# Second block's attention as six two-head jobs between weight units, bias as tiles from DRAM

## The chip, the cores and the metric

One of the cores of a Trainium2 chip runs the kernel. The metric is the device time of one execution in microseconds; less is better.

## What is computed

Two different transformer blocks of two layers each run on 256 rows of 1024 numbers, all in fp32. The first has four kinds of attention and an MLP. The second, in which the change lies, projects x by `w_in_2` (11,648 columns) and has two mixers side by side. One is attention in three groups of six heads of 64 (windows 128, 512, 2048, dilations 1, 4, 16) with a T5 bias by distance:

```
s = einsum(q, k) * 64 ** -0.5 + bias[bucket(distance)]; masked outside window and dilation
o = softmax(s) v per group; y_a = sum over groups of softmax(lse over groups) * o
```

Since the groups are merged by their log denominators, the three groups of a head are one softmax over 3 x 256 keys. The other mixer is retention in four heads (query and key 256, value 512), whose queries and keys are rotated by position. Both mixers are projected and gated, then come `w_out_2`, LayerNorm, a SwiGLU and another LayerNorm.

## The kernel before

**Weights in three products.** TensorE works in fp32r. A weight unit is 512 rows by 512 columns (1 MB). SP loads it into one of four buffers `raw`, ScalarE copies it to `whi` (helper `hi`, line 1007), VectorE subtracts to `wlo` (`lo`, line 1386), and TensorE multiplies for four blocks of k and two row tiles: x high and x low by `whi` (lines 573, 574), x high by `wlo` (line 579), 24 matmuls of 512 columns. A chunk of w_in is two units into a pair of PSUM banks; VectorE adds the input bias and stores it (`project`, line 1744). `whi` and `wlo` have two buffers each, so hi of a unit waits for the unit two before it.

**Order.** Each engine has its program written out by hand, with counting semaphores (`Tally`). In a layer of the second block TensorE turns x (`first_chunk`), makes chunks 0 to 5 of w_in (queries, keys, part of the values), turns queries and keys (line 598, 36 transposes), makes chunk 6, and then runs attention alone: `run_jobs` with `JOBS2`, 12 jobs, one for each head and row tile m. Job step q has `logits2` of job q, `job_turn` of job q - 1 and `job_outputs` of job q - 2. Then YA, the attention's output, is turned, and the ten units of chunks 7 to 11 follow (7 to 10 are the queries and keys of retention). Then retention's blocks are turned (`T2_RET`).

**A job.** For each of three groups TensorE multiplies a 64 row block of queries with (m + 1) x 128 keys (line 720), and adds the bias by two matmuls against a reversed identity, `flip` (line 723). Its operands, the high and low part of a skewed read of the bias rows in DRAM, are loaded by SP for each job into `YH` and `YL`, behind a wait for the logits two jobs before. VectorE takes the row maximum (line 1425) and negates it (line 1427), ScalarE does the exponential from PSUM (line 1007), TensorE turns the probabilities into PSUM tile `T` (two banks, line 598), VectorE copies them (line 1448), TensorE multiplies with the values into `A` (line 641), and VectorE divides by the sum (lines 1455, 1457).

**Retention's rotation** is `rotate` on VectorE (lines 1773 to 1780), after each of chunks 7 to 10, with its scratch `RTR` in the arena.

**Setup.** One matmul (line 662) and some VectorE operations make the 18 bias rows from `rel_bias_2`; ScalarE writes them to DRAM early. GpSimd loads constants, `decay` among them, and rotates some heads of the first block. In the first block the logits (line 691) of a job come from four heads, with neighbours in different row halves, the transposes have line 598 and the value matmuls line 646.

## Time and profile before

| | |
|---|---|
| Runs, median of 3 | 2182.11 us (2181.06 to 2182.19) |
| The profiled execution, its own time | 2180.04 us |
| Its span | 2178.2 us |
| Mean granted TensorE clock | 0.922 |
| Busy, share of the span: TensorE, VectorE, ScalarE, GpSimd | 94%, 55%, 40%, 3% |
| DMA, mean over the span | 158 GB/s |

Engines are PE (TensorE, with PEld for its weight loads), DVE (VectorE), ACT (ScalarE), POOL (GpSimd) and SP. The granted clock is a share of full speed. Busy TensorE is not TensorE at its best: its matmuls take longer at a lower clock. An fp32 matmul is two records in the trace, an fp32r matmul one; in the first block's groups "x8" are four fp32 matmuls. Numbers behind the bar of a group are idle time before it and what ended it.

### The profile page before, as it was taken

To read this page: it belongs to the slowest core of one execution; us is meant where nothing else is said; L and a number is where in the kernel's file an instruction comes from. 1 tells how busy PE (TensorE), PEld (TensorE's weight loads), DVE (VectorE), ACT (ScalarE), POOL (GpSimd) and SP (SyncE) were. 2 spreads that over 40 slices of the span, in tenths; PEclk is the share of its full clock that TensorE was granted. 3 is DMA by queue.
4 is the path that set the end of the run, shared out by engine and by line. 5 is a ranking of instruction groups with operands and counts; after the bars stand their busy time and mean duration, and the time that the engine had idled before them with its cause. 6 is when DMAs were issued, how large, how long until landed. Compare 5 with 4: busy or idle time off the path is not lost.

```text
span 2178.2 us, 26315 instructions
## 1 busy us (share of the span) xinstructions
PE 2043.5 (94%) x9270; PEld 1672.1 (77%) x9270; DVE 1193.5 (55%) x1360; ACT 873.9 (40%) x997; POOL 62.1 (3%) x88
## 2 busy tenths in 40 slices
PE   4998999899899998999999989997999999998997
PEld 3886888687778877877877778886877887787885
DVE  3675555557555555433766564445532757555455
ACT  3544444456253444311345434443321335443442
POOL 2210000022000000000000000000000000000000
PEclk9987999999799999956999999998965999999998
DMA  5413555452245544643655645554644555654553
GB/s 192 148 52 121 177 189 173 156 168 90 77 155 180 192 150 157 207 87 108 209 177 174 208 145 169 179 183 165 205 113 126 173 175 174 193 187 132 177 180 115
DMA packets 214819, 345.17 MB, mean 158 GB/s; under 512 B 13355, under 2 KB 82219, under 8 KB 214721
## 3 DMA queue, kind: packets, MB, share of 16 engines
q1 hardware_dynamic: 213440, 342.10, 49.4%
q8 instruction: 58, 0.95, 0.2%
q0 software_dynamic: 384, 1.31, 0.2%
q10 hardware_dynamic: 897, 0.49, 0.1%
q14 instruction: 40, 0.33, 0.1%
HBM read 342.74 MB, written 1.12 MB: 158 GB/s over the span
## 4 chain that ended last, share of the span: by engine, by line
PE 86%; DVE 5%; issue 3%; DVEq 3%; ACT 2%; POOL 0%; POOLq 0%; ACTq 0%
PE G L573 21%; PE G L574 21%; PE G L579 20%; PE T L598 5%; PE A L573 3%; PE A L574 3%; PE A L579 3%; PE G L720 3%; PE G L723 2%; PE A L641 2%; DVE wlo L1386 1%; ACT arena L1007 1%; PE A L646 1%; DVEq L1431 1%; ACT whi L1007 1%
## 5 line engine op out<-in xcount | busy, mean ns | idle before, releaser
L1386 DVE TENSOR_TENSOR wlo<-raw,whi 128x2048 fp32r<-128x2048 f32 (+3 forms) x320 | 676.5, 2116 | 661.3 <-ACT whi L1007 661.1
L1007 ACT ACTIVATE whi<-raw 128x2048 fp32r<-128x2048 f32 (+3 forms) x320 | 565.9, 1769 | 789.0 <-PE G L579 718.5
L573 PE MATMUL G<-whi,XH 128*128 128x512 f32 x1696 | 680.1, 401 | 6.6 <-DVE XL L1401 6.6
L574 PE MATMUL G<-whi,XL 128*128 128x512 f32 x1696 | 669.7, 395 | 0.0
L579 PE MATMUL G<-wlo,XH 128*128 128x512 f32 x1696 | 419.3, 389 | 0.0
L573 PEld LDWEIGHTS G<-whi,XH 128*128 128x128 f32 x1696 | 325.0, 192 | 77.0 <-issue 6.4
L574 PEld LDWEIGHTS G<-whi,XL 128*128 128x128 f32 x1696 | 324.6, 191 | 68.1 <-issue 1.9
L579 PEld LDWEIGHTS G<-wlo,XH 128*128 128x128 f32 x1696 | 318.2, 188 | 66.9 <-DVE wlo L1386 0.7
L598 PE MATMUL T<-ident,arena 128*128 128x128 f32 x812 | 136.8, 313 | 25.9 <-ACT arena L1007 19.3
L598 PEld LDWEIGHTS T<-ident,arena 128*128 128x128 f32 x812 | 109.0, 161 | 44.4 <-ACT arena L1007 18.5
L1007 ACT ACTIVATE arena<-G,nm 128x128 f32<-128x128 f32 (+2 forms) x104 | 50.3, 493 | 196.0 <-DVE nm L1427 151.2
L598 PE MATMUL T<-ident,X 128*128 128x128 f32 x160 | 34.2, 382 | 73.8 <-DVEq L1531 20.6
L573 PE MATMUL G<-whi,MH 128*128 128x512 f32 x240 | 96.1, 400 | 5.4 <-DVE ML L1401 5.4
L574 PE MATMUL G<-whi,ML 128*128 128x512 f32 x240 | 94.9, 395 | 0.0
L598 PEld LDWEIGHTS T<-ident,X 128*128 128x128 f32 x160 | 26.6, 196 | 83.1 <-issue 53.0
L573 PE MATMUL A<-whi,MH 128*128 128x512 f32 x216 | 84.0, 389 | 0.0
L574 PE MATMUL A<-whi,ML 128*128 128x512 f32 x216 | 84.0, 389 | 0.0
L1425 DVE TENSOR_REDUCE mx<-G 128x1 f32<-128x384 f32 (+1 forms) x24 | 18.2, 758 | 95.9 <-PE G L723 95.9
L720 PE MATMUL G<-arena 64*128 64x128 f32 (+1 forms) x144 | 69.2, 580 | 0.0
L579 PE MATMUL G<-wlo,MH 128*128 128x512 f32 x240 | 61.3, 389 | 0.0
L1007 ACT ACT_TABLE_LOAD x42 | 53.9, 1283 | 14.0 <-issue 11.0
L573 PEld LDWEIGHTS G<-whi,MH 128*128 128x128 f32 x240 | 46.1, 192 | 15.8 <-issue 5.9
(187 smaller groups left out, 1882.2 us busy)
## 6 DMA issues: line engine op xcount, KB each, us to landing
raw<-in_w_in SPq DMA_DIRECT2D x112, 1024.0 KB, 7.0
raw<-in_w_mlp_up SPq DMA_DIRECT2D x32, 1024.0 KB, 5.4
raw<-in_w_mlp_down SPq DMA_DIRECT2D x32, 1024.0 KB, 5.0
raw<-in_w_ffn_gate SPq DMA_DIRECT2D x44, 512.0 KB, 4.1
raw<-in_w_ffn_up SPq DMA_DIRECT2D x44, 512.0 KB, 5.0
raw<-in_w_ffn_down SPq DMA_DIRECT2D x44, 512.0 KB, 3.3
raw<-in_w_out SPq DMA_DIRECT2D x16, 1024.0 KB, 5.0
raw<-in_w_ret_proj SPq DMA_DIRECT2D x16, 1024.0 KB, 5.1
```

The source lines that it names most:

```text
L573: nc.tensor.matmul(dst(m), hx[:, k0 + k, rows], hi[:, k, :], start=first and k == 0, stop=False)
L574: nc.tensor.matmul(dst(m), lx[:, k0 + k, rows], hi[:, k, :], start=False, stop=False)
L579: mm = nc.tensor.matmul(dst(m), hx[:, k0 + k, m * P:(m + 1) * P], lo[:, k, :], start=False, stop=last and k == kb - 1)
L598: tr = nc.tensor.transpose(T[:, t % 2, n * P:(n + 1) * P], src, ident[:])
L641: mm = nc.tensor.matmul(A[:, q % 2, 0:HD], PT2[:, q % 2, kt, u * P:(u + 1) * P], v, start=(u == 0 and kt == 0), stop=(u == 2 and kt == m))
L646: mm = nc.tensor.matmul(A[:, q % 2, u * HD:(u + 1) * HD], PT[:, q % 2, kt, u * P:(u + 1) * P], Z[:, kt, col:col + HD], start=kt == 0, stop ...
L720: nc.tensor.matmul(dst[:, g, 0:n], QT2[part, b, m * P:(m + 1) * P], QT2[part, 9 + b, 0:n], start=True, stop=False)
L723: mm = nc.tensor.matmul(dst[:, g, 0:n], flip[:], BR[b_part][:, 3 * (q % 2) + g, 0:n], start=False, stop=b_part == 1)
L1007: return nc.scalar.activation(out_, in_, func, **kw)
L1386: tt(wlo[:, c % PARTS, 0:n], raw[:, slot, 0:n], whi[:, c % PARTS, 0:n].bitcast(F32), ALU.subtract).then_inc(s_lo.sem, 1)
L1425: nc.vector.tensor_reduce(mx[:, q, 0:1], logit_set(q)[:, 0:3, 0:n], AX.XY, ALU.max)
L1431: dve.drain()
```

## The change

Attention becomes six jobs, for three pairs of heads and two row tiles. The two heads of a pair lie in the two row halves; their logits matmuls alternate and go to different banks. The bias is not multiplied any more: GpSimd writes each of the 18 rows 128 times to DRAM (after its work for the first block), and reads it back skewed as tiles of 128 x 6 x 256, three per layer, on its own queue. VectorE's tensor_tensor_reduce adds the tile to the logits, stores the sum to SBUF and gives the maximum. ScalarE does the exponential there and also the copies of the turned probabilities. The heads' output goes to the first columns of a bank of `T`. The first eight of retention's units run between the steps, into `A`; YA is turned between units 8 and 9. The rotations run between the steps too, with their scratch in `gains`, so that the LayerNorm's gains are loaded later. `decay` first holds the bias rows and is loaded after them. `flip`, its load and the split of the rows go; query and key part of z and the values have rooms of their own.

```diff
-JOBS2 = [("E", m, h) for h in range(HG) for m in range(TILES)]
+JOBS2 = [("E", m, pair) for pair in range(HG // 2) for m in range(TILES)]
+ATT_UNITS = 8
...
-    bias_rows = nc.dram_tensor("bias_rows", (2, 18, 512), F32R, kind="Internal").ap()
+    bias_rows = nc.dram_tensor("bias_rows", (18, P, 512), F32, kind="Internal").ap()
...
-        PT2 = room(13056, 2, TILES, 384)
+        PT2 = room(13824, 2, 1, 384), room(14592, 2, TILES, 384)
+        YA = room(16128, TILES, YA_W)
-        RTR = room(13056, 2, TILES, 2, P)
+        RTR = gains[:].rearrange("p a b -> p (a b)")[:, 0:1024].rearrange("p (a m h d) -> p a m h d", a=2, m=TILES, h=2)
...
-                sp.wait_ge(s_x.sem, s_x.at(1, L, 0))
-                for n, name in enumerate(("ln1_g_2", "ln1_b_2")):
-                    sp.dma_start(gains[:, n:n + 1, :], a[name][bass.ds(L, 1), :].partition_broadcast(P)).then_inc(
-                        s_gain.sem, 16)
                 w_in_chunks(0, V_RET, 7, RQ0, 1)
-                sp.wait_ge(s_brow, 32)
-                sp.wait_ge(s_t.sem, s_t.at(1, L, T2_QK))
-                for q, (_, m, h) in enumerate(JOBS2):
-                    if q >= 2:
-                        sp.wait_ge(s_log.sem, s_log.at(1, L, q - 1))
-                    n = (m + 1) * P
-                    for part in range(2):
-                        src = bass.AP(bias_rows.tensor, (18 * part + h) * 512 + (1 - m) * P,
-                                      [[1, P], [HG * 512, 3], [1, n]]).bitcast(F32)
-                        sp.dma_start(BR[part][:, 3 * (q % 2):3 * (q % 2) + 3, 0:n].bitcast(F32), src).then_inc(s_br[q % 2].sem, 16)
                 with sp.Fori(0, 3) as i:
                     w_in_chunks(i, V_RET + 2, 8, RQ0 + COLS)
                 w_in_chunks(0, V_RET + 14, 14, RQ0 + 7 * COLS, 1)
                 with sp.Fori(0, 4) as i:
                     w_in_chunks(i, V_GATE, 15, RQ0 + 8 * COLS)
+                sp.wait_ge(s_rot.sem, s_rot.at(1, L, 4))
+                for n, name in enumerate(("ln1_g_2", "ln1_b_2")):
+                    sp.dma_start(gains[:, n:n + 1, :], a[name][bass.ds(L, 1), :].partition_broadcast(P)).then_inc(
+                        s_gain.sem, 16)
                 for n in range(2):
...
+        def logit_set(q, x):
+            m = JOBS2[q][1]
+            n = (m + 1) * P
+            g = G[:, 2 * x:2 * x + 2, :].rearrange("p b s -> p (b s)")
+            return g[:, 0:3 * n].rearrange("p (g s) -> p g s", g=3)
+        def heads_out(q):
+            return T[:, (T2_JOB + job_end(JOBS2, q)) % 2, 0:P]
...
+                        for g in range(3):
+                            for kt in range(m + 1):
+                                mm = nc.tensor.matmul(heads_out(q)[:, h * HD:(h + 1) * HD],
+                                                      PT2[m][:, h, kt, g * P:(g + 1) * P],
+                                                      ZV[:, kt, (g * HG + 2 * x + h) * HD:][:, 0:HD],
+                                                      start=g == 0 and kt == 0, stop=g == 2 and kt == m)
+                    mm.then_inc(s_pv.sem, 1)
+                    return
...
+            def pair_turn(L, q, kt):
+                m = JOBS2[q][1]
+                pe.wait_ge(s_exp.sem, s_exp.at(1, L, q + 1))
+                pe.wait_ge(s_o.sem, s_o.at(1, L, q))
+                for h in range(2):
+                    t = T2_JOB + job_banks(JOBS2, q) + 2 * kt + h
+                    transposes(1, L, 0, t, [PR2[m][:, h, g, kt * P:(kt + 1) * P] for g in range(3)])
...
             def logits2(L, q):
-                _, m, h = JOBS2[q]
+                _, m, j = JOBS2[q]
                 n = (m + 1) * P
-                part = slice(HD * (h % 2), HD * (h % 2) + HD)
-                pe.wait_ge(s_exp.sem, s_exp.at(1, L, q - 1))
-                pe.wait_ge(s_br[q % 2].sem, s_br[q % 2].at(1, L, q // 2 + 1))
-                dst = logit_set(q)
+                pe.wait_ge(s_nm.sem, s_nm.at(1, L, q))
                 for g in range(3):
-                    b = 3 * g + h // 2
-                    nc.tensor.matmul(dst[:, g, 0:n], QT2[part, b, m * P:(m + 1) * P], QT2[part, 9 + b, 0:n],
-                                     start=True, stop=False)
-                    for b_part in range(2):
-                        mm = nc.tensor.matmul(dst[:, g, 0:n], flip[:], BR[b_part][:, 3 * (q % 2) + g, 0:n],
-                                              start=False, stop=b_part == 1)
+                    for h in range(2):
+                        part = slice(HD * h, HD * (h + 1))
+                        b = 3 * g + j
+                        mm = nc.tensor.matmul(logit_set(q, h)[:, g, :], QT2[part, b, m * P:(m + 1) * P],
+                                              QT2[part, 9 + b, 0:n], start=True, stop=True)
                 mm.then_inc(s_log.sem, 1)
...
-                pe.wait_ge(s_evac.sem, s_evac.at(1, L, 6))
-                run_jobs(1, L, JOBS2, T2_JOB, logits2, PR2, v_there)
-                pe.wait_ge(s_o.sem, s_o.at(1, L, len(JOBS2)))
-                turn(1, L, 0, T2_YA, Z2, 3, per=1)
+                turn(1, L, 0, T2_QK, ZQK, 18)
+                chunk(1, L, 0, 12, 0, LAST2)
+                def ya_turn(L):
+                    pe.wait_ge(s_o.sem, s_o.at(1, L, len(JOBS2)))
+                    turn(1, L, 0, T2_YA, YA, 3, per=1)
+                def ret_unit(u):
+                    if u == 0:
+                        pe.wait_ge(s_tfree.sem, s_tfree.at(1, L, T2_JOB))
+                    elif u % 2 == 0:
+                        pe.wait_ge(s_evac.sem, s_evac.at(1, L, SEG1 + u // 2))
+                    unit(1, L, 0, V_RET + u, XH, XL, UK * (u % 2), UK, COLS, bank_pair(2), u % 2 == 0, u % 2 == 1)
+                ret_unit(0)
+                pe.wait_ge(s_evac.sem, s_evac.at(1, L, SEG1))
+                for q in range(len(JOBS2) + 2):
+                    if q >= 2:
+                        job_outputs(1, L, q - 2, JOBS2, T2_JOB)
+                    if q < len(JOBS2):
+                        logits2(L, q)
+                    if 1 <= q <= len(JOBS2):
+                        for kt in range(JOBS2[q - 1][1] + 1):
+                            pair_turn(L, q - 1, kt)
+                    if q + 1 < ATT_UNITS:
+                        ret_unit(q + 1)
...
-                with pe.Fori(0, 2) as i:
-                    for c in range(2):
-                        w_in_chunk(i, SEG1 + c, V_RET + 2 * c)
-                w_in_chunk(0, 11, V_RET + 8)
+                second_chunk(1, L, V_RET + 8, lambda: ya_turn(L), 1)
+                pe.wait_ge(s_tfree.sem, s_tfree.at(1, L, T2_RET))
                 pe.wait_ge(s_rot.sem, s_rot.at(1, L, 4))
...
+            def pair_exps(L, q):
+                m = JOBS2[q][1]
+                act.wait_ge(s_nm.sem, s_nm.at(1, L, q + 1))
+                for h in range(2):
+                    ins = act_(PR2[m][:, h], PR2[m][:, h], ACT.Exp, bias=nm[:, q, h:h + 1], scale=SCALE["E"],
+                               accum_out=ls[:, q, h:h + 1])
+                ins.then_inc(s_exp.sem, 1)
+            def pair_copies(L, q):
+                m = JOBS2[q][1]
+                for kt in range(m + 1):
+                    for h in range(2):
+                        t = T2_JOB + job_banks(JOBS2, q) + 2 * kt + h
+                        act.wait_ge(s_t.sem, s_t.at(1, L, t + 1))
+                        act_(PT2[m][:, h, kt], T[:, t % 2, 0:384], ACT.Copy).then_inc(s_tfree.sem, 1)
...
-                    exps(1, L, q, JOBS2, PR2)
-                    if q in (2, 4):
-                        hi(1, L, 0, 13 + q // 2)
+                his(1, L, 0, V_RET, V_RET + 1)
+                for q in range(len(JOBS2) + 2):
+                    if 1 <= q <= len(JOBS2):
+                        pair_copies(L, q - 1)
+                    hi(1, L, 0, V_RET + 2 + q)
+                    if q < len(JOBS2):
+                        pair_exps(L, q)
+                hi(1, L, 0, V_RET + 10)
                 turn_hi(1, L, 0, T2_YA, 3, MH, per=1)
-                with act.Fori(0, 2) as i:
-                    his(1, L, i, V_RET + 2, V_RET + 3, V_RET + 4, V_RET + 5)
-                hi(1, L, 0, V_RET + 10)
...
+            pool.wait_ge(s_bvec, 1)
+            for g in range(3):
+                pool.dma_start(bias_rows[g::3], rowsb_of(g).unsqueeze(1).to_broadcast([HG, P, 512])).then_inc(s_brow, 16)
+            pool.wait_ge(s_brow, 48)
+            pool.dma_start(decay[:], a["c_decay"]).then_inc(s_dec, 16)
+            with pool.Fori(0, DEPTH) as L:
+                def bias_tiles(j, free):
+                    pool.wait_ge(*free)
+                    pool.sem_inc(s_tile, 1)
+                    src = bass.AP(bias_rows.tensor, 6 * j * P * 512 + P - 1, [[511, P], [P * 512, 6], [1, S]])
+                    pool.dma_start(BR[j % 2][:, 0:6, :].bitcast(F32), src).then_inc(s_br[j % 2].sem, 16)
+                bias_tiles(0, (s_t.sem, s_t.at(1, L, T2_QK)))
+                bias_tiles(1, (s_t.sem, s_t.at(1, L, T2_QK)))
+                bias_tiles(2, (s_nm.sem, s_nm.at(1, L, 2)))
...
+                _, m, j = JOBS2[q]
+                if m == 0:
+                    dve.wait_ge(s_br[j % 2].sem, s_br[j % 2].at(1, L, j // 2 + 1))
+                dve.wait_ge(s_log.sem, s_log.at(1, L, q + 1))
+                dve.sem_inc(s_seen, 1)
+                for h in range(2):
+                    bias = BR[j % 2][:, 3 * h:3 * h + 3, P * (1 - m):S].bitcast(F32)
+                    nc.vector.tensor_tensor_reduce(PR2[m][:, h], logit_set(q, h), bias, 1.0, 2 * NEG, ALU.add, ALU.max,
+                                                   mx[:, q, h:h + 1])
+                dve.drain()
+                ts(nm[:, q, 0:2], mx[:, q, 0:2], -SCALE["E"], None, ALU.mult).then_inc(s_nm.sem, 1)
+            def pair_outputs(L, q):
+                _, m, j = JOBS2[q]
+                dve.wait_ge(s_pv.sem, s_pv.at(1, L, q + 1))
+                nc.vector.reciprocal(rl[:, q, 0:2], ls[:, q, 0:2])
+                dve.drain()
+                tt(YA[:, m, 2 * j * HD:2 * (j + 1) * HD].rearrange("p (h d) -> p h d", h=2),
+                   heads_out(q).rearrange("p (h d) -> p h d", h=2),
+                   rl[:, q, 0:2].unsqueeze(2).to_broadcast([P, 2, HD]), ALU.mult).then_inc(s_o.sem, 1)
...
-                with dve.Fori(0, 2) as i:
-                    for c in range(2):
-                        los(1, L, i, V_RET + 2 + 2 * c, V_RET + 3 + 2 * c)
-                        project(i, SEG1 + c, QK[:, :, bass.ds(i * 1024 + c * COLS, COLS)])
+                los(1, L, 0, V_RET, V_RET + 1)
+                dve.wait_ge(s_dec, 16)
+                for q in range(len(JOBS2) + 2):
+                    c = q // 2
+                    if q >= 2:
+                        pair_outputs(L, q - 2)
+                    if q % 2:
+                        project(0, SEG1 + c, QK[:, :, c * COLS:(c + 1) * COLS])
+                    if q < len(JOBS2):
+                        pair_prep(L, q)
+                    lo(1, L, 0, V_RET + 2 + q)
+                    if q % 2:
                         dve.drain()
-                        rotate(i, c).then_inc(s_rot.sem, 1)
+                        rotate(0, c).then_inc(s_rot.sem, 1)
+                lo(1, L, 0, V_RET + 10)
+                turn_lo(1, L, 0, T2_YA, 3, MH, ML, per=1)
```

## Rows read from the trace of the kernel before

**Rows 1.** The page: granted TensorE clock in 40 slices of the span, tenths of full speed.
```profile
PEclk9987999999799999956999999998965999999998
```

**Rows 2.** Windows: length, busy us (records) of PE, PEld, DVE, ACT, POOL; PEclk, DMA, GB/s.
```profile
925.00:1009.00 84.00, 83.96 (x287) 64.55 (x285) 29.95 (x65) 13.10 (x26) 0.00 (x0) 0.50 0.51 124
921.20:1069.30 148.10, 146.86 (x553) 115.62 (x553) 71.59 (x109) 32.01 (x38) 0.00 (x0) 0.69 0.46 123
1590.40:1738.40 148.00, 146.80 (x554) 115.68 (x554) 71.62 (x109) 32.01 (x38) 0.00 (x0) 0.69 0.45 124
```

**Rows 3.** Groups of instructions, attention of layer 0, 921.2 to 1012.5 us: busy us, mean ns.
```profile
L720 PE MATMUL G<-arena 64*128 64x128 f32 (+1 forms) x72 | 34.5, 579 | 0.0
...
L723 PE MATMUL G<-YH,flip 128*128 128x128 f32 (+1 forms) x36 | 18.3, 509 | 0.0
...
L723 PE MATMUL G<-YL,flip 128*128 128x128 f32 (+1 forms) x36 | 14.4, 400 | 0.0
...
L1448 DVE COPY arena<-T 128x384 f32<-128x384 f32 x18 | 10.0, 558 | 0.2
...
L1007 ACT ACTIVATE arena<-G,nm 128x384 f32<-128x384 f32 (+1 forms) x12 | 8.9, 741 | 75.6 <-DVE nm L1427 75.6
L1386 DVE TENSOR_TENSOR wlo<-raw,whi 128x2048 fp32r<-128x2048 f32 x2 | 4.6, 2280 | 0.0
L1007 ACT ACTIVATE whi<-raw 128x2048 fp32r<-128x2048 f32 x2 | 3.8, 1898 | 0.0
...
L1744 DVE TENSOR_TENSOR arena<-A,swap 128x768 f32<-128x768 f32 x1 | 0.9, 948 | 0.0
```

**Rows 4.** Timeline of PE, attention of the first block: start us, busy us.
```profile
157.70 0.71 PE L691 MATMUL G<-arena 64*128 64x128 f32 x8
158.35 0.40 PE L695 MATMUL G<-maskb,identb 128*128 128x128 bf16 x4
159.19 1.09 PE L598 MATMUL T<-ident,arena 128*128 128x128 f32 x8 [0.45 <-ACT arena L1007]
160.12 1.90 PE L646 MATMUL A<-arena 128*128 128x64 f32 x16
161.95 1.13 PE L691 MATMUL G<-arena 64*128 64x256 f32 x8
163.02 0.62 PE L695 MATMUL G<-maskb,identb 128*128 128x128 bf16 x8
165.22 0.65 PE L598 MATMUL T<-ident,arena 128*128 128x128 f32 x4 [1.58 <-ACT arena L1007]
```

**Rows 5.** Timeline of PE, last groups of two neighbouring units of w_in.
```profile
1687.62 1.98 PE L579 MATMUL G<-wlo,XH 128*128 128x512 f32 x8
...
1693.06 1.98 PE L579 MATMUL G<-wlo,XH 128*128 128x512 f32 x8
```

**Rows 6.** Timeline of DVE, one operation of a rotation.
```profile
1031.57 0.69 DVE L1773 TENSOR_TENSOR arena<-arena,rot 128x512 f32<-128x512 f32 x1 [0.20 <-issue]
```

**Rows 7.** Busy time by windows around idle times of TensorE.
```profile
128.10:137.80 9.70, 8.99 (x84) 7.76 (x84) 7.15 (x15) 4.61 (x12) 3.33 (x8) 1.00 0.00 0
137.80:139.90 2.10, 0.00 (x0) 0.00 (x0) 1.86 (x7) 1.96 (x9) 0.00 (x0) 0.99 0.00 0
143.40:156.60 13.20, 13.20 (x61) 10.87 (x61) 9.90 (x21) 3.37 (x12) 0.00 (x0) 0.50 0.01 2
1223.00:1225.20 2.20, 0.35 (x3) 0.10 (x1) 1.89 (x3) 1.88 (x1) 0.00 (x0) 1.00 0.57 126
1225.20:1229.00 3.80, 3.80 (x10) 3.02 (x11) 3.43 (x2) 0.03 (x1) 0.00 (x0) 0.55 0.68 219
```

**Rows 8.** The window from the last GpSimd work to the next weight loads.
```profile
534.00:585.00 51.00, 41.41 (x247) 35.98 (x248) 36.88 (x83) 19.15 (x63) 0.00 (x0) 0.69 0.00 1
```

**Rows 9.** DMA issues: count, KB each, median us from issue to landing.
```profile
YH<-bias_rows SPq DMA_DIRECT2D x12, 384.0 KB, 5.3
```

**Rows 10.** The window of the transposes of the query and key blocks.
```profile
907.00:912.70 5.70, 4.86 (x36) 3.68 (x35) 1.23 (x1) 4.29 (x8) 0.00 (x0) 1.00 1.01 378
```

124 lines of the change are left out of this document (45 added, 79 removed).

## The prediction, made before the change was run

> **What bounds the kernel now.** The page comes first. Its row of the granted TensorE clock has two deep dips, one a little before the middle and one at three quarters [rows 1]. The attention of the second block is there, once for each of the two layers. The windows come next: from the first logits to the last matmul of w_in chunk 11, the stretch that the change rebuilds, the layers take 148.1 and 148.0 us. In 84 us of the first one the granted clock is 0.50, the lower of its two levels (1.2 and 2.4 GHz), and TensorE is busy for 83.96 of these 84 us [rows 2]. So nothing waits here for VectorE or ScalarE: TensorE is the bound, at half speed. Last, the groups of the attention part show what it does there. The logits have 34.5 us busy for 36 matmuls (an fp32 matmul is two records, so 72), and the matmuls against the flip matrix that stand behind each of them 18.3 + 14.4 [rows 3].
>
> **The new stretch at full clock.** It holds the same ten weight units, 36 logits matmuls, 54 transposes and 54 value matmuls, and the 6 transposes of YA; the flips are gone. The prices come from the first block, where the same shapes run at clock 1.00 with heads that alternate between the row halves [rows 4].
> - Units: the last groups of two neighbours start 5.44 us apart [rows 5], so 10 x 5.44 = 54.4.
> - Logits: four matmuls of 64x128 take 158.35 - 157.70 = 0.65 us, four of 64x256 take 163.02 - 161.95 = 1.07, which is 0.16 and 0.27 each: 18 x 0.16 + 18 x 0.27 = 7.7. Now all run in the same row half, 34.5 us at half clock, about 17.3 at full. That is the upper bound, if the halves don't overlap. I take 7.7, since shape and alternation are the same.
> - Transposes: eight in 0.93 us, 0.116 each: 60 x 0.116 = 7.0.
> - Value matmuls: eight (16 records) in 1.83 us, 0.23 each: 54 x 0.23 = 12.4.
>
> Sum 81.5 us of TensorE.
>
> **Waits that take their place.** Count from the end of the logits of an odd step (a job with m = 1). VectorE prepares two heads, does lo of one unit (2.3 us), and rotates. ScalarE first has the copies of two turned banks, then hi (1.9) [rows 3]. The preparation is a tensor_tensor_reduce, which the trace does not show. Its nearest row adds a PSUM and an SBUF operand over 768 elements, 0.95 us [rows 3]. Two heads and the small negation are 2.2 us at once this price, which I take as the row that it is nearest to, and 4.1 at twice; less than once is excluded, as the elements are read. The copies (0.56 each by VectorE's, [rows 3]) end at about 1.3, hi at 3.2, lo at 5.5. The rotation, six operations of 0.69 with small overlaps [rows 6], ends at 9.6, and only then comes the output of the job before, 0.6 with its reciprocal, at 10.2. TensorE turns two banks (0.7), runs a unit (5.4), the value matmuls of an m = 0 job (1.4) and its logits (1.0), and stands before the next turn at 8.5. That turn writes the bank in which the heads' output lies and waits for VectorE to take it: 1.7 us in two even steps, 2.7 in the third, where no logits are left. The three are 6.1 us; at twice the preparation 3.5 more. The same turn fills four groups into two banks, so the third and the fourth wait for ScalarE's copies, some 0.4 each time, 1.3 in all. Before unit 9 comes the YA turn. Its third bank needs hi of the next unit (1.9), its lo (2.3) and the split of the first bank (some 0.8), all after unit 8: 5.0 us.
>
> 81.5 + 6.1 + 1.3 + 5.0 = 94 us at full clock.
>
> **What the clock takes.** An idle time of 1.6 us ended the mixture of [rows 4], and one of 2.1 (137.8) that of [rows 7]; 1.85 at 1223 was enough as well. In each case the clock went to 0.50 at its end or a few us on. Gaps of 0.7 in all, from 128.1 to 137.8, left it at 1.00. After 1223 a unit needed 3.8 us at the lower level before the clock rose [rows 7], so 1.9 lost. I take 2.5, as here a turn at half speed comes before the unit, for the three waits and for YA: 10 us. The new stretch is 104 us, the gain 148 - 104 = 44 per layer, 88 in all.
>
> **The rest, at nothing.** The weight loads no longer stand on SP behind 24 bias transfers and their waits. Eight units of 1 MB in some 85 us ask for about 100 GB/s, and the stretch moved 123 [rows 2]. GpSimd writes the rows in three transfers of 1.57 MB after its last work, at about 534 us; until 585 the DMA engines stand still [rows 8], and the first reader comes after 830, so the cover is some 300 us. Then it loads decay again, needed at 921. The bias tiles are 0.79 MB, three per layer, on GpSimd's queue. Two are asked for at the layer's start, some 80 us early. The third has from the second job's preparation to the fifth's, over 20 us; by 384 KB in 5.3 us [rows 9] it takes 11. Without that cover its time would stand in step 4, in front of everything. The LayerNorm gains now wait on SP for the fourth rotation, behind the gate chunks' loads. It is over by then, and the attention projection queued behind waits for free buffers anyway. The bank copies go from VectorE to ScalarE, which in two steps has 2 hi, 6 copies and 4 exponentials (0.74 each, [rows 3]), about 10 us in 22. At the start VectorE loses three small operations, but the first XH waits for GpSimd's chain: nothing.
>
> The sum is 2180.0 (the profiled execution; its span is 2178.2) - 88 = 2092. The median of the runs is 2.1 above that execution, so 2094.
>
> **A rule that speaks against it.** The clock stayed at 1.00 from 907.0 to 912.7, where TensorE did nothing but 36 transposes with short gaps [rows 10]. The Trainium skill, "TensorE: Matmul & The Clock Gate", section "Part 4: PE-mode transpose", says that a transpose does not count as activity for the clock in the way a matmul does. By that rule the attention parts would look idler than they are, and the clock would fall in each; the trace disagrees. The rivals below rest on other rows.
>
> **Rivals.**
> 1. The clock is held: VectorE's waits come out under about a microsecond. Then 94 us per layer, 2180 - 108 + 2 = 2074. For: from 128.1 to 137.8 such a mixture kept 1.00. Against: what ended it. 12 in 100.
> 2. A fall in every attention part, not in three: four more at 2.5 make 114 us, and 117.5 with the dearer preparation: 2114 to 2121. For: 143.4 to 156.6, dense small matmuls that stayed at 0.50 [rows 7]. Halves that don't overlap, the change not doing what it says, end here too: 104 + 9.6. 22 in 100.
> 3. The clock stays low all through the attention parts, and each unit regains it only on its way. The small matmuls double to 54 us, units are 5.4 + 2 = 7.4, with YA 54 + 74 + 5 = 133 us: 2180 - 30 + 2 = 2152. For: 84 us at 0.50 now. Against: these held flips and one-sided logits. 8 in 100.
> 4. Slower: the clock stays low through the units too. They take 10.9 each, 54 + 109 + 5 = 168 us, 20 more than now per layer: 2222. It decides from the point where 94 + (low time)/2 passes 148, at 108 us of low clock in the stretch. Against: units alone brought the clock back after 1225. 5 in 100.
> 5. No change within the error, by a late tile or weight that eats the gain. 3 in 100.
>
> The forecast has 50 in 100. The range reaches from below the first rival to above the second with the dearer preparation, 2066 to 2134, and leaves out about 16 in 100. A measurement of this kernel tells 0.2% (4 us) from no change. Faster 0.92, within 0.2% 0.03, slower 0.05.
>
> **What would show it.** In the changed profile: stretches of about 104 us; no flips; pairs of logits matmuls at 0.16 and 0.27 us each; three waits of TensorE per layer for VectorE's output of a job, and one of 5 us at YA; low clock only behind these, so that the mean over the stretch is above 0.85. Wrong would be a mean below 0.75, a tensor_tensor_reduce of 768 elements over 1.5 us, or waits for bias tiles or weights.

## The result, and the profile of the changed kernel

The changed kernel takes **2085.9 us** (median of 4 runs, 2085.01 to 2086.5), the kernel before 2181.59 (median of 4, 2178.89 to 2182.19): a ratio of 0.9567, 95% interval 0.9556 to 0.9578, so 95.7 us less where 88 were forecast. The profiled execution took 2086.5 us with a span of 2084.7; before it was 2180.0 and 2178.2.

The page's row of the granted clock, to be read against [rows 1]:

```profile
PEclk9988999999779999999999999999999999999998
```

The two deep dips are gone. The one left, in the two slices from 521 to 625 us, lies in the first block's layer 1, whose own work the change leaves as it was; the third window below and [rows 8] have a clock of 0.67 and 0.69 there. Next the windows of the rebuilt stretch, from its first retention unit to the end of the last one, in layer 0 and layer 1, and then the window of [rows 8]. Columns as in [rows 2]:

```profile
923.60:1023.50 99.90, 88.28 (x482) 73.59 (x481) 59.13 (x85) 36.87 (x55) 0.83 (x1) 0.93 0.40 128
1544.60:1644.60 100.00, 88.36 (x481) 73.56 (x480) 59.14 (x85) 36.87 (x55) 0.83 (x1) 0.93 0.40 127
534.00:585.00 51.00, 41.72 (x240) 36.27 (x239) 36.49 (x82) 17.90 (x58) 1.93 (x2) 0.67 0.73 86
```

148 us became 100, at a mean clock of 0.93. In the third row the DMA engines, which stood still before, are 0.73 busy.

The timeline of PE in layer 0: start, busy, and in brackets the idle time before it with its releaser.

```profile
929.12 0.94 PE L733 MATMUL G<-arena 64*128 64x128 f32 x12
935.68 1.57 PE L733 MATMUL G<-arena 64*128 64x256 f32 x12
943.37 1.45 PE L642 MATMUL T<-arena 128*128 128x64 f32 x12
947.56 3.01 PE L599 MATMUL T<-ident,arena 128*128 128x128 f32 x12 [1.88 <-DVE arena L1503]
956.11 2.79 PE L642 MATMUL T<-arena 128*128 128x64 f32 x24
970.70 0.91 PE L599 MATMUL T<-ident,arena 128*128 128x128 f32 x6 [1.87 <-DVE arena L1503]
971.83 1.54 PE L599 MATMUL T<-ident,arena 128*128 128x128 f32 x6 [0.22 <-ACT arena L1030]
994.03 0.87 PE L599 MATMUL T<-ident,arena 128*128 128x128 f32 x6 [2.77 <-DVE arena L1503]
1016.39 0.69 PE L599 MATMUL T<-ident,arena 128*128 128x128 f32 x2 [4.64 <-DVE ML L1448]
```

These are the four forecast waits: three turns for VectorE's output of a job (L1503), one for the low part of YA (L1448). Windows of 1 us show the clock falling to the lower level behind each of them, at 947 to 951, 971 to 975, 995 to 999 and 1015 to 1019, and nowhere else in the stretch. The new operations of VectorE in the same window, from the groups of instructions with each shape apart (busy, mean ns | idle before):

```profile
L1492 DVE CUSTOM_DVE_ANT_0 arena<-G,YH 128x768 f32<-128x768 f32 x4 | 3.7, 956 | 0.3 <-PE G L733 0.3
L1492 DVE CUSTOM_DVE_ANT_1 arena<-G,YH 128x384 f32<-128x384 f32 x4 | 2.1, 555 | 1.2 <-PE G L733 1.1
L1503 DVE TENSOR_TENSOR arena<-T,rl 128x128 f32<-128x128 f32 x6 | 1.7, 292 | 0.4
```

The tensor_tensor_reduce appears as CUSTOM_DVE and costs 0.956 us for 768 elements.

Two turns of X mark off the part of layer 0 that holds the stretch: the first turn of the second block, and the turn of the SwiGLU's input in the same layer. They are given for the changed kernel, then for the kernel before:

```profile
808.51 1.09 PE L599 MATMUL T<-ident,X 128*128 128x128 f32 x8 [0.53 <-DVE X L1601]
...
1254.32 1.96 PE L599 MATMUL T<-ident,X 128*128 128x128 f32 x8 [6.02 <-DVE X L1959]
```

```profile
805.92 1.09 PE L598 MATMUL T<-ident,X 128*128 128x128 f32 x8 [0.55 <-DVE X L1548]
...
1300.12 1.96 PE L598 MATMUL T<-ident,X 128*128 128x128 f32 x8 [6.02 <-DVE X L1897]
```

They stand 445.8 us apart where they stood 494.2, so layer 0's stretch gains 48.4. The rest of the span, which holds the end of layer 0 and the whole of layer 1, takes 830.4 where it took 878.1: 47.7. Together 96.1, and the span fell by 93.5, so up to 808 us the kernel has lost 2.6. That has two parts. The first unit of the program starts 2.4 us earlier (34.06 for 36.42), and 1.8 of it are still there at the first turn of the first block's layer 1 (402.05 for 403.83). That layer then loses 1.8 + 2.6 = 4.4. The view of the line that issues the bias row writes shows who waited for them:

```profile
L1408 POOL DMA_DIRECT2D bias_rows<-decay x3: 1067/1085/1205, 532.6 to 534.9; - x3
...
who waited for it (us, times):
  POOL decay L1410: 65.9, 1
```

The timeline of ScalarE:

```profile
604.68 1.91 ACT L1030 ACTIVATE whi<-raw 128x2048 fp32r<-128x2048 f32 x1 [7.74 <-DMA raw<-in_w_mlp_up]
```

And that of PE, for the changed kernel and for the kernel before:

```profile
613.31 1.96 PE L599 MATMUL T<-ident,X 128*128 128x128 f32 x8 [7.44 <-DVE X L1601]
```

```profile
610.76 1.86 PE L598 MATMUL T<-ident,X 128*128 128x128 f32 x8 [3.45 <-DVE X L1548]
```

The writes are issued from 532.6 us on, and GpSimd, which waits for all of them, goes on at 601.9, 65.9 us behind the end of the last issue. ScalarE sits idle for 7.74 us until a weight of the MLP lands, and behind that weight's copy stand its reads of the results that the next turn needs. That turn waits 7.44 us; before it waited 3.45. That the writes are the reason is tested below.

### The profile page after: what moved, and what is told of

It reads as the page before. It is cut to its first block, busy times and chain, and to the rows that moved or that the text cites. A ratio compares the mean times of both kernels' runs of the same rounds, so it can differ in the third digit from the quotient of the medians.

```text
span 2084.7 us, 25827 instructions
## 1 busy us (share of the span) xinstructions
PE 1924.9 (92%) x9126; PEld 1586.0 (76%) x9126; DVE 1165.3 (56%) x1311; ACT 887.3 (43%) x1033; POOL 69.2 (3%) x97
## 4 chain that ended last, share of the span: by engine, by line
PE 80%; DVE 7%; issue 4%; DVEq 4%; ACT 3%; DMA 1%; SPq 0%; POOL 0%; POOLq 0%; ACTq 0%
PE G L574 20%; PE G L575 20%; PE G L580 19%; PE T L599 5%; PE A L574 4%; PE A L575 4%; PE A L580 4%; DVE wlo L1433 2%; ACT whi L1030 1%; ACT arena L1030 1%; PE A L652 1%; DVEq L1473 1%; PE T L642 1%; DMA raw<-in_w_mlp_up 1%; DVE SCO L1636 1%
## 5 line engine op out<-in xcount | busy, mean ns | idle before, releaser
L574 PE MATMUL G<-whi,XH 128*128 128x512 f32 (+1 forms) x1600 | 640.7, 400 | 6.6 <-DVE XL L1448 6.6
L575 PE MATMUL G<-whi,XL 128*128 128x512 f32 (+1 forms) x1600 | 629.7, 394 | 0.0
L580 PE MATMUL G<-wlo,XH 128*128 128x512 f32 (+1 forms) x1600 | 393.9, 388 | 0.0
L574 PEld LDWEIGHTS G<-whi,XH 128*128 128x128 f32 x1600 | 306.5, 192 | 71.9 <-issue 6.4
L575 PEld LDWEIGHTS G<-whi,XL 128*128 128x128 f32 x1600 | 306.0, 191 | 63.0 <-issue 1.9
L580 PEld LDWEIGHTS G<-wlo,XH 128*128 128x128 f32 x1600 | 299.7, 188 | 62.0 <-DVE wlo L1433 0.9
L599 PE MATMUL T<-ident,arena 128*128 128x128 f32 x812 | 126.6, 299 | 49.3 <-ACT arena L1030 21.3
L574 PE MATMUL G<-whi,MH 128*128 128x512 f32 x240 | 96.1, 400 | 5.4 <-DVE ML L1448 5.4
L1030 ACT ACTIVATE arena<-T 128x512 f32<-128x512 f32 (+2 forms) x92 | 47.0, 550 | 114.1 <-PE T L599 112.8
L574 PE MATMUL A<-whi,XH 128*128 128x512 f32 (+1 forms) x224 | 93.0, 416 | 0.0
L575 PE MATMUL A<-whi,XL 128*128 128x512 f32 (+1 forms) x224 | 89.4, 400 | 0.0
```

What stands on the lines that cost most here:

```text
L574: nc.tensor.matmul(dst(m), hx[:, k0 + k, rows], hi[:, k, :], start=first and k == 0, stop=False)
L575: nc.tensor.matmul(dst(m), lx[:, k0 + k, rows], hi[:, k, :], start=False, stop=False)
L580: mm = nc.tensor.matmul(dst(m), hx[:, k0 + k, m * P:(m + 1) * P], lo[:, k, :], start=False, stop=last and k == kb - 1)
L599: tr = nc.tensor.transpose(T[:, t % 2, n * P:(n + 1) * P], src, ident[:])
L1030: return nc.scalar.activation(out_, in_, func, **kw)
```

## The experiments

Each was timed beside the kernel before on the same chip; times are medians. Unless the text says otherwise, an edit is shown against the changed kernel. The letters A, B and C are the theories of the expectation that stands ahead of each result. The changed kernel itself, run once more:

> The changed kernel itself, once more and on the same chip as the run beside it, so that the two can be set against each other: 2083 to 2088 us, as in its first four executions.

**2086.39 us** (5 runs, 2085.35 to 2091.27), ratio 0.9573 (0.956 to 0.9586).

### One rotation later

```diff
-                    if q % 2:
+                    if q and q % 2 == 0:
                         dve.drain()
-                        rotate(0, c).then_inc(s_rot.sem, 1)
+                        rotate(0, c - 1).then_inc(s_rot.sem, 1)
+                dve.drain()
+                rotate(0, 3).then_inc(s_rot.sem, 1)
                 lo(1, L, 0, V_RET + 10)
```

> VectorE's rotation of a pair of retention columns (4.0 us) moves from the odd step, where it stands ahead of the output of the job before, into the next even step behind that step's output and weight low part; the last rotation stands where the last low part begins. Theory A (the three idle times of TensorE of 1.88, 1.87 and 2.77 us per layer end with the output of VectorE, which stands behind this rotation, and each also costs a fall of the clock of about 1.7 us): they go, or fall below 1 us, with the three falls of the clock; 6 us of waits and 3 x 1.7 us of clock per layer less what comes in their place (the output is 0.5 to 1 us late even so): 8 to 11 us per layer, 2064 to 2070 us, and the stretch takes about 90 us. Rival B (TensorE waits for something else that becomes ready at the same time, a transpose bank or ScalarE): the waits stay over 1.5 us with another releaser, 2082 to 2087 us. Rival C (the waits go, but the clock falls in the attention parts nevertheless): 6 us per layer, 2072 to 2076 us. The wait of 4.64 us at the turn of YA stays in all of them, or grows by the last rotation to 5 to 7 us.

**2069.59 us** (2065.45 to 2070.92), ratio 0.9485 (0.9467 to 0.9503). The window of the stretch of layer 0:

```profile
924.60:1016.70 92.10, 85.35 (x481) 70.58 (x480) 58.93 (x85) 36.42 (x55) 0.83 (x1) 0.96 0.44 138
```

The two long waits that are left in it, from the timeline of PE:

```profile
987.23 0.87 PE L599 MATMUL T<-ident,arena 128*128 128x128 f32 x6 [0.81 <-DVE arena L1503]
...
1008.55 0.69 PE L599 MATMUL T<-ident,arena 128*128 128x128 f32 x2 [5.18 <-DVE ML L1448]
```

Theory A holds: the first two waits are gone, the third fell from 2.77 to 0.81, and the clock falls only at YA, from 1007 to 1014. From turn to turn (808.51 to 1245.84) layer 0 takes 437.3 us, 8.5 less.

### And YA ahead of the last weight

The edit against the run above, ScalarE's part and VectorE's:

```diff
-                hi(1, L, 0, V_RET + 10)
                 turn_hi(1, L, 0, T2_YA, 3, MH, per=1)
+                hi(1, L, 0, V_RET + 10)
...
-                dve.drain()
+                turn_lo(1, L, 0, T2_YA, 3, MH, ML, per=1)
                 rotate(0, 3).then_inc(s_rot.sem, 1)
                 lo(1, L, 0, V_RET + 10)
-                turn_lo(1, L, 0, T2_YA, 3, MH, ML, per=1)
```

> As the one before, and the high and low parts of the attention's output YA are made by ScalarE and VectorE ahead of the last weight's high and low part and of the last rotation. Theory A (the wait of 4.64 us at the turn of YA, for VectorE's low part, is the order of VectorE's queue and nothing else): it falls below 1.5 us and the fall of the clock behind it goes too; 4 to 6 us per layer below the one before, 2052 to 2062 us, and the retention's low part of the last unit is not late since a unit stands before it. Rival B (what stands behind the turn, the last weight's low part or the rotation, is late in its place): a wait of 3 us or more at the retention's first turn or at the unit that uses the last low part, and 2062 to 2070 us, no better than the one before.

**2056.61 us** (2051.91 to 2057.01), ratio 0.9432 (0.9416 to 0.9448). The window of the stretch:

```profile
919.50:1004.60 85.10, 82.81 (x481) 68.78 (x480) 57.22 (x85) 36.44 (x55) 0.83 (x1) 1.00 0.46 149
```

The turn of YA, from the timeline of PE:

```profile
998.86 0.44 PE L599 MATMUL T<-ident,arena 128*128 128x128 f32 x2 [0.72 <-DVE ML L1448]
```

Theory A again. The stretch is 85.1 us at a clock of 1.00 throughout, 14.8 less than in the changed kernel. TensorE's busy time is 82.81 us, beside the 81.5 of the prediction's sum at full clock. So the order of VectorE's and ScalarE's queues explained the waits, and the waits the falls of the clock. This profile is of the quickest of the four executions, 2051.91 us. Its second block begins at 804.35 where the changed kernel's begins at 808.51, so most of its lead on the median was won ahead of the stretch and has nothing to do with the edit.

### The row halves apart

```diff
-                for g in range(3):
-                    for h in range(2):
+                for h in range(2):
+                    for g in range(3):
```

> The six logits of a query tile are issued all of the upper row half first and then all of the lower, so that no two neighbours work on different halves of TensorE's rows; nothing else differs. In the trace of the changed kernel twelve logits of 256 columns in alternation take 1.57 us and twelve of 128 columns 0.94 us, so the 36 of a layer cost 7.7 us of the stretch of about 100 us (923.6 to 1023.6 in layer 0). Theory A (the alternation halves the price of a logit, and the clock falls only behind the four idle times of 1.88, 1.87, 2.77 and 4.64 us): the logits cost up to 10.8 us more per layer at full clock, of which the three waits for VectorE's output give back up to 4.5, since VectorE has that much more time; 2 x 4 to 2 x 8 us more, 2092 to 2102 us, with the three idle times under 1 us. Rival B (a long run of matmuls that use half of the rows lowers the clock by itself): the granted clock falls in the attention parts themselves, the windows of the stretch show a mean under 0.7 where it was about 0.85, and the time is 2108 to 2122. Rival C (the halves overlap wherever they stand, or the price of a logit is not what counts): logits unchanged, 2084 to 2088.

**2088.42 us** (2082.44 to 2091.44), ratio 0.9575 (0.9551 to 0.9599). It can't be told from the changed kernel. The timeline shows the logits of an m = 0 and an m = 1 job, and the first two waits for VectorE:

```profile
929.55 1.26 PE L733 MATMUL G<-arena 64*128 64x128 f32 x12
936.43 2.10 PE L733 MATMUL G<-arena 64*128 64x256 f32 x12
...
948.85 0.87 PE L599 MATMUL T<-ident,arena 128*128 128x128 f32 x6 [1.55 <-DVE arena L1503]
...
971.36 0.96 PE L599 MATMUL T<-ident,arena 128*128 128x128 f32 x6 [1.57 <-DVE arena L1503]
```

All three theories missed in part. The halves do overlap in alternation, but a logit without it costs only a third more: 1.26 and 2.10 us for six (12 records) where 0.94 and 1.57 stood, 3 x 0.32 + 3 x 0.53 = 2.6 us a layer. The expectation allowed 10.8. The prediction's upper bound of 17.3 came from halving the 34.5 us of [rows 3], where each logit stood between two matmuls of all 128 rows. Of the 2.6, shorter waits gave back 0.6 (1.55 and 1.57 for 1.88 and 1.87), and the stretch grew by 1.9. The logits themselves did not bring the clock down (1.00 from 924 to 972): rival B is out. The first wait, 1.55 us, left the clock at 1.00 too; the second, 1.57 us, brought it down from 972 to 976.

### The units behind the jobs

```diff
-                    if q + 1 < ATT_UNITS:
-                        ret_unit(q + 1)
+                for u in range(ATT_UNITS):
+                    ret_unit(u)
```

with the banks, weight parts and rotations in the order that goes with it.

> The six attention jobs keep their form (two heads of two row halves each, bias tiles from DRAM, 36 logits of up to 256 columns), but the eight retention units of w_in that stood between their steps are all issued behind them. Theory A (the gain of about 48 us per layer has two parts: fewer and paired instructions, and the units as cover for the chain of softmax on ScalarE and VectorE and for the clock): TensorE waits at each step for exp, output and value, the attention runs at the lower of the two clocks nearly throughout (in the kernel before it did over its attention part, [rows 2]), and the stretch takes about 120 us where it now takes 100; 2 x 16 to 2 x 24 us more, 2118 to 2134 us, the low-clock time of the stretch 40 us or more per layer. Rival B (the gain comes from the removed bias matmuls and copies alone, and the order of units and jobs is worth nothing): 2084 to 2092 us, the stretch within 3 us of 100.

**2108.80 us** (2107.12 to 2116.24), ratio 0.9682 (0.9658 to 0.9706), between the two theories. The windows show the six jobs by themselves, and a piece of 25 us of them:

```profile
925.00:969.40 44.40, 33.23 (x235) 27.89 (x236) 16.22 (x42) 18.33 (x43) 0.83 (x1) 0.83 0.23 72
935.00:960.00 25.00, 20.37 (x168) 17.19 (x168) 9.49 (x33) 13.02 (x32) 0.83 (x1) 1.00 0.12 33
```

The timeline of PE shows what TensorE waits for there:

```profile
930.60 2.93 PE L733 MATMUL G<-arena 64*128 64x256 f32 x12 [4.58 <-DVE nm L1494]
935.26 1.55 PE L642 MATMUL T<-arena 128*128 128x64 f32 x12 [0.63 <-ACT arena L1030]
...
960.77 0.96 PE L599 MATMUL T<-ident,arena 128*128 128x128 f32 x6 [1.41 <-ACT arena L1030]
```

The cover that units give is real: without it TensorE is idle for 11.2 us of 44.4, and layer 0 takes 9.8 us more from turn to turn. But the expectation that attention alone runs at the lower clock nearly throughout was wrong. The clock was low at the entry (927 to 935) and again from 961 to 972, behind an idle time of 1.41 us; between them, with idle times of up to 0.63 us, it stayed at 1.00.

### What held the clock down before

Three runs ask why the old attention part ran at 0.50 [rows 2]. The first leaves out the flip matmuls of the kernel before, the second its logits.

```diff
-                    for b_part in range(2):
-                        mm = nc.tensor.matmul(dst[:, g, 0:n], flip[:], BR[b_part][:, 3 * (q % 2) + g, 0:n],
-                                              start=False, stop=b_part == 1)
```

with the stop flag of the logits that goes with it.

> The kernel before without the two matmuls against the flip matrix behind each logit (72 a layer), which leaves the relative bias out of the second block's attention. They had 18.3 + 14.4 = 32.7 us busy per layer at a granted clock of 0.50 [rows 3]. Theory A (what keeps the clock at 0.50 for 84 us is the mixture of logits of one row half with these matmuls, two weights loaded for each short product; it is not one-sidedness alone, since the changed kernel with its halves apart kept 1.00): without them the attention part runs at full clock but for some falls behind waits, and takes 40 to 50 us in place of 84 and more; stretch 100 to 110 us where it was 148, time 2096 to 2112 us. Rival B (the one-sided logits keep the clock low by themselves, and only the small reordering of heads in the changed kernel frees it): clock still about 0.50, the part 84 - 33 = 51 us and more with waits; stretch 115 to 120, time 2116 to 2126.

**2131.78 us** (2129.83 to 2133.72), ratio 0.9781 (0.9752 to 0.9809).

```diff
-                    nc.tensor.matmul(dst[:, g, 0:n], QT2[part, b, m * P:(m + 1) * P], QT2[part, 9 + b, 0:n],
-                                     start=True, stop=False)
```

with the start flag of the first flip matmul that goes with it.

> The kernel before without the logits proper (36 matmuls of 64 rows a layer), so that the relative bias alone makes the softmax of the second block's attention. They had 34.5 us busy per layer at a granted clock of 0.50 [rows 3]. Theory A (the mixture holds the clock down, not either kind by itself): full clock with falls behind waits, stretch 100 to 112 us, time 2096 to 2116 us. Rival B (the matmuls against the flip matrix hold it down by themselves): clock about 0.50 through the part, the stretch 148 - 34 = 114 us or more, time 2112 to 2126 us.

**2110.07 us** (2108.06 to 2112.09), ratio 0.9681 (0.9653 to 0.9709). Windows of the first, then of the second:

```profile
926.00:990.00 64.00, 61.69 (x233) 52.94 (x234) 28.74 (x66) 13.06 (x25) 0.00 (x0) 0.50 0.62 154
```

```profile
928.00:960.00 32.00, 30.88 (x144) 30.41 (x145) 19.02 (x42) 9.27 (x16) 0.00 (x0) 0.50 0.72 139
```

Theory A of the first fell: without flips the clock still stayed at the lower level for 64 us, and the time is above even rival B's. In part that is a wait of TensorE for the bias rows, 3.43 us, which the kernel before doesn't have; from the timeline of PE:

```profile
926.04 1.64 PE L720 MATMUL G<-arena 64*128 64x128 f32 x6 [3.43 <-DMA YL<-bias_rows]
```

The second's time lies in A's range, but for another reason: windows of 1 us show its clock at 0.50 up to 960, then at 1.00, and at 0.50 again from 967 to 984. Both kinds of matmul can stand at 0.50 without the other. The last run joins the units behind and the halves apart:

> Both single edits together: the eight retention units behind the six jobs, and the six logits of a tile issued one row half after the other. With the units between the steps the second edit cost 2 us of a stretch and no clock; with the units behind, and the halves in alternation, the granted clock was 1.00 from 935 to 960 us. The kernel before without its flip matmuls, all logits of a job in one half and no units between, stayed at 0.50 from 926 to 990. Theory A (in attention alone, alternation is what lets the clock rise again after the idle time at its entry): the clock stays near 0.50 for 40 us or more of the attention part, which takes 60 us or more where it took 44.4; 2 x 15 to 2 x 20 us above the 2108.8 of the run with the units behind, 2136 to 2150 us. Rival B (the clock rises with the new jobs whatever the order of halves; what held it down before lies elsewhere, in the smaller jobs): the part takes 45 to 48 us, 2109 to 2116 us.

**2114.05 us** (2110.88 to 2117.22), ratio 0.9696 (0.9661 to 0.973). Its jobs by themselves:

```profile
925.00:971.40 46.40, 38.49 (x236) 32.32 (x237) 13.28 (x43) 17.70 (x42) 0.83 (x1) 0.83 0.19 63
```

And one idle time in them, from the timeline of PE:

```profile
962.99 0.87 PE L599 MATMUL T<-ident,arena 128*128 128x128 f32 x6 [1.40 <-ACT arena L1030]
```

Rival B: the clock fell at 924, rose at 941, and stayed, even behind these 1.40 us. So alternation isn't what frees it; at most it shortens the low level at the entry, 17 us here for 7 (927 to 934) in the run with the units behind. What in the new jobs lets the clock rise where the old ones, in the first of these runs at least, did not within 64 us, stays open: the new jobs differ in several things at once, and no run takes these one by one.

### The writes of the bias rows

First held, then cut to the columns that are read:

```diff
             pool.wait_ge(s_bvec, 1)
+            pool.wait_ge(s_hi.sem, s_hi.at(0, DEPTH - 1, U_MLP + 4))
```

> GpSimd holds its three writes of the bias rows (1536 KB each) until the first block's layer 1 has the high part of its fifth MLP weight, some 98 us later (about 632 instead of 532.6 us of the span). Theory A (in the changed kernel these writes, on their way from 532.6 to 601, are what makes the weight of the MLP land 7.7 us late for ScalarE, and TensorE's wait at 613 grow from 3.45 us in the kernel before to 7.44): the wait is 3.4 to 3.6 us again, that turn stands 4 us earlier (about 609.3), and since the MLP behind 620 moves its 184 GB/s of weights in only 0.57 of the queues' time, the writes fit in beside it; 3 to 5 us less, 2081 to 2083 us. Rival B (the writes delay weights wherever they stand): the wait at 609 goes but other waits for a weight of 3 us or more in all come at 640 to 720; 2084 to 2090 us. Rival C (the wait of 7.44 us has another cause): it stays, 2085 to 2087 us.

**2107.27 us** (2106.82 to 2109.39), ratio 0.9669 (0.9655 to 0.9682). From the timeline of PE:

```profile
609.17 1.14 PE L599 MATMUL T<-ident,X 128*128 128x128 f32 x5 [3.45 <-DVE X L1602]
671.28 0.79 PE L574 MATMUL G<-whi,XH 128*128 128x512 f32 x1 [15.86 <-ACT whi L1030]
701.50 0.75 PE L574 MATMUL G<-whi,XH 128*128 128x512 f32 x1 [4.09 <-ACT whi L1030]
```

And a window of 20 us ahead of the longest wait:

```profile
640.00:660.00 20.00, 15.43 (x73) 12.52 (x71) 5.91 (x4) 3.23 (x4) 0.00 (x0) 1.00 0.98 168
```

The wait at 609 is 3.45 again and stands 4.1 us earlier, so the writes were its cause (A). But B came seven times as large as it was priced: 15.86, 1.48 and 4.09 us of new waits, 21 us more in all. The writes took 0.73 of the engines' time for 86 GB/s in the changed kernel, the weights of this part 0.57 for 184. The sum is 1.30. By it they could not fit, and two rows would have said so. In the window of 20 us the share is 0.98.

The second edit, by itself:

```diff
-                pool.dma_start(bias_rows[g::3], rowsb_of(g).unsqueeze(1).to_broadcast([HG, P, 512]))
+                pool.dma_start(bias_rows[g::3, :, 0:384], rowsb_of(g)[:, 0:384].unsqueeze(1).to_broadcast([HG, P, 384]))
```

> Each bias row is written with 384 of its 512 columns (the tiles read only the first 383), so the three writes carry a quarter less and stand where they stood. Theory A (the time of the writes, 66 us from the first issue to the last landing, goes with their bytes, and the late weight with their end): the last lands after some 50 us, at about 583, only 1 us after the first MLP weight of the layer is asked for; the wait at 613 is 3.5 to 5 us where it was 7.44, 2 to 4 us less, 2082 to 2084 us. Rival B (the time goes with the number of rows written, 2304, and not with their bytes): the last write lands at 598 to 601 as before, the wait stays at 7 to 7.5 us, 2085 to 2087 us.

**2082.18 us** (2079.16 to 2083.51), ratio 0.9552 (0.9539 to 0.9565). Who waited for the writes:

```profile
  POOL decay L1410: 49.5, 1
```

The turn, from the timeline of PE:

```profile
605.91 1.97 PE L599 MATMUL T<-ident,X 128*128 128x128 f32 x8 [3.45 <-DVE X L1601]
```

Theory A: the time went with the bytes (49.5 us behind the last issue for 65.9, with three quarters of them), and the wait is that of before. The time by itself would not show it: the interval of the ratio overlaps the changed kernel's. This profile too is of the quickest execution, 2079.16 us, so its turn stands earlier than the wait alone explains.

### All of it

> The rotations and the order at YA as in the run with both of them, the writes held and with 384 columns. If the two savings are independent (they stand in different stages, the one in the second block of each layer, the other once at 613 us): the 2056.6 us of that run less 3 to 5, 2051 to 2054 us, against the kernel before a ratio of 0.941. Rival (a MLP step that takes the weights sooner finds another resource late, or the held writes disturb the steps behind 632 us): no better than 2056.

**2069.62 us** (2068.01 to 2070.61), ratio 0.9491 (0.9478 to 0.9504): the rival. It is 13 us above the run with both moves, so holding the writes costs more than it saves even at 384 columns (a wait of 13.61 us at 669.69). So the last version has both moves and 384 columns, but doesn't hold:

> The rotations and the order at YA as in the run with both of them, and the bias rows written with 384 columns where the changed kernel writes them (issued at about 532 us), not held. If the two savings add (14.7 us per layer in the second block, and 3.5 to 4 us at the turn of the first block's layer 1, whose wait goes from about 7.5 to 3.45 us since the last row lands before that layer's MLP weights are under way): 2056.6 less 3.5 to 4, 2050 to 2054 us, a ratio of 0.9405 to 0.942. Rival (the saving at that turn is taken back by the spread between executions or by a later wait): 2055 to 2058 us.

**2051.07 us** (2050.2 to 2053.11), ratio 0.9409 (0.9396 to 0.9422), 35.3 us below the changed kernel on the same chip, within the expected range and the fastest here. The turn that the writes had held up waits 3.45 us again, from the timeline of PE:

```profile
610.25 1.61 PE L599 MATMUL T<-ident,X 128*128 128x128 f32 x8 [3.45 <-DVE X L1601]
```

Its ratio's interval just overlaps that of the run with both moves and 512 columns, so the 5.5 us between them are not a measure of the writes.

## Why the prediction held, step by step

The time, 2085.9, is 8.1 us below the forecast of 2094 and well inside its range; the likeliest case was the one that came. For the profiled execution the forecast was 2092, and it took 2086.5: 5.5 less, 8.1 by the stretches and -2.6 by terms that were counted at nothing. The other 2.7 us are spread between executions: the forecast put the median 2.1 above the profiled one, and it came out 0.6 below it.

- **The bound.** TensorE at half speed in [rows 2] was the cost. Taken apart by the runs, in one order of several: without flips alone 2179.2 became 2131.8 (47 us); the new jobs, with the units behind, 2108.8 (23 more, and they hold the bias, which the run without flips lacks; pairing, bias tiles and ScalarE's copies come together in this step and were not taken apart); the units between them 2085.9 (23 more). Alternation is at most 3 of these.
- **TensorE at full clock, 81.5.** In the stretch 88.28 us are busy at a mean clock of 0.93. The two levels are 1.00 and 0.50, so a mean of 0.93 means that (1 - 0.93) x 99.9 = 7.0 us of them went to the lower one, and 81.3 is left. Logits at 0.16 and 0.27 were right. Their upper bound of 17.3 was too high: one half after the other takes 18 x 0.21 + 18 x 0.35 = 10.1.
- **The waits.** Forecast 1.7, 1.7, 2.7 and 5.0; they were 1.88, 1.87, 2.77 and 4.64. The tensor_tensor_reduce, taken from a tensor_tensor over as many elements at 0.95, was 0.956, and 0.555 for 384. The waits for ScalarE's copies, forecast at 1.3 in all, came out smaller: the stretch has 99.9 - 88.28 = 11.6 us of idle time, the four waits are 11.2 of it, and 0.4 to 0.5 is left for everything else. Moving the rotation took two of the first three away and left 0.81 of the third; moving YA left 0.72 of the fourth. One price of the prediction does not follow from its own queue: a preparation at twice the price lets lo end at 4.1 + 2.3 = 6.4 and not 5.5, 0.9 later each time, so 2.7 us more and not 3.5. Only the upper end of rival 2 hangs on it.
- **The clock, mis-sized.** The four falls stood where they were put, but cost 7.0 / 4 = 1.75 us each, not 2.5. That is 3 of the 4 us by which a stretch beat the forecast of 104. The price of 1.9 that [rows 7] gave was nearer than the surcharge put on it for a turn at half speed.
- **The rule against it.** The forecast set aside the rule of the Trainium skill, "TensorE: Matmul & The Clock Gate", section "Part 4: PE-mode transpose", for [rows 10]. By it the clock would fall in each attention part. In the version with both moves it fell in none, in 85.1 us with 60 transposes; with the units behind it stood at 1.00 for 25 us of attention alone, 36 transposes and 5.3 of 20.4 busy us. The traces disagree once more, though neither holds transposes alone as [rows 10] does.
- **"The rest, at nothing" failed in two steps.** The start was counted at nothing and gave 2.4 us. GpSimd's row writes were given a cover of "some 300 us", from their issue at 534 to the first reader. That is a cover for the reader alone. What they collided with were the weight loads after 585, where the window of [rows 8] ends; the writes lasted until 601.9, and that layer of the first block lost 4.4 us. Held or cut to 384 columns, they left its wait at 3.45. The bias tiles landed in 6.2 and 7.6 us (medians of the two buffers), under the estimate of 11, and nobody waited for them.
- **The ledger.** Layers 48.4 + 47.7 for 88, what is left of the start 1.8, the writes -4.4: 93.5 of span.
- **The rivals.** A held clock (1) needed waits under a microsecond. That is what the version with both moves has, and its time fits the mechanism: a stretch of 85.1 us, below the 94 since the waits themselves are gone. Falls in every attention part (2), and a low clock throughout (3, 4), did not come, not even with the halves apart. With the units behind, attention stood low at its entry and its end only. That the first two waits brought the clock down was nearer to luck than the forecast's four falls suggest: at 1.88 and 1.87 us they were not far above the 1.55 that left it up in the run with the halves apart.

## What to carry to other kernels

Price a change of order by writing out each engine's queue between two waits: here it gave four waits within 0.4 us, and the same list pointed at two moves that brought another 29 us. A transfer "at nothing" needs two covers, for its reader and for every queue that runs before it has landed. Add the DMA shares of what would overlap: 0.73 + 0.57 is more than 1, and the run that put them together lost 21 us.

## What the runs showed that was not expected

- Three writes to DRAM of 1536 KB from a source repeated over 128 rows took 65.9 us from the end of the last issue until the engine that waits for them went on, and 49.5 with three quarters of the bytes. They load the DMA engines heavily for what they move: 0.73 of their time for 86 GB/s, where weights took 0.57 for 184.
- At full clock a logit of 64 rows costs 0.21 us (128 columns) and 0.35 us (256) among its like in one row half, and 0.16 and 0.26 in alternation. By that 36 logits of one half take 10.1 us; half of what they took between matmuls of all rows was 17.3.
- The clock can stay at its lower level for 64 us in which TensorE is busy for 61.69 (the kernel before without flips), and at the higher for 25 us in which it is busy for only 20.37 (the units behind). Busy time by itself did not order these cases.
- In the stretches shown here idle times of TensorE of 1.87 us and more came with a fall of the clock each time, and those up to 0.81 us never. Between them it went either way: 1.40 us (halves apart and units behind) and 1.55 (halves apart) left it at 1.00, and 1.41 (units behind) and 1.57 (halves apart) brought it down. So a wait of about 1.5 us can't be priced to better than one fall, some 1.75 us.
